# Attention: the scores of the next unit are issued ahead of a stage's product with the values

## The reference, cut to what matters

```python
# group B, 8 heads: three dilated windows (128,1), (512,4), (2048,16), each a softmax, merged
s = einsum(q, k) * SCALE;  p, lse = masked_softmax(s, mask);  o = einsum(p, v)
# group A, 8 heads in 2 groups of 4: compressed blocks, selected blocks, sliding window of 512
s = einsum(q, kc) * SCALE; p_cmp, _ = masked_softmax(s, ...);  o_cmp = einsum(p_cmp, vc)
top, idx = top_k(score from p_cmp)                             # which key blocks are looked at
s = einsum(q, ks) * SCALE; p, _ = masked_softmax(s, ms);       o_slc = einsum(p, vs)
s = einsum(q, kw) * SCALE; p, _ = masked_softmax(s, window);   o_win = einsum(p, vw)
o = g0 * o_cmp + g1 * o_slc + g2 * o_win
```

## Time and profile before

| | us |
|---|---|
| median of 3 runs | 2145.36 (2137.95 to 2154.14) |
| the profiled execution | 2156.45 |
| its span, first to last instruction | 2154.6 |
| attention: PE's first turn to its last product | 548.8 to 1160.2 |
| PE busy in the span | 1894.2 (88%) |
| DVE busy | 1111.1 (52%) |
| ACT busy | 821.7 (38%) |
| POOL busy | 272.2 (13%) |

### The profile page before, as it was taken

The page is one execution under the profiler, slowest core; times in us unless marked ns, Lnnn a source line. Parts: engine busy times, 40 slices in busy tenths (PEclk is TensorE's granted clock), DMA queues, the critical chain, the costliest instruction groups (busy, mean ns, idle before and its releaser), DMA issues. The chain is left out here.

```text
span 2154.6 us, 29729 instructions
## 1 busy us (share of the span) xinstructions
PE 1894.2 (88%) x10915; PEld 1555.6 (72%) x10915; DVE 1111.1 (52%) x2627; ACT 821.7 (38%) x1742; POOL 272.2 (13%) x342
## 2 busy tenths in 40 slices
PE   3998996457799868888884999999999999999997
PEld 3787775456688757777673778788778878878885
DVE  4776861122678757776774433443344344344344
ACT  4444431100678756665664323222123122222211
POOL 0000000101344434443431000000000000000000
PEclk9999997688899999999997999999999999999998
DMA  5322213661465523222224311220231121133102
GB/s 176 110 76 101 81 51 58 85 118 40 130 168 157 151 71 107 82 84 82 84 94 127 123 59 59 98 71 28 97 98 59 40 98 59 40 98 127 32 18 87
DMA packets 172326, 189.93 MB, mean 88 GB/s; under 512 B 55942, under 2 KB 139110, under 8 KB 171000
## 3 DMA queue, kind: packets, MB, share of 16 engines
q1 hardware_dynamic: 170114, 187.13, 29.9%
q10 hardware_dynamic: 2080, 1.05, 0.2%
HBM read 166.60 MB, written 59.81 MB: 105 GB/s over the span
## 5 line engine op out<-in xcount | busy, mean ns | idle before, releaser
L2419 DVE SCALAR_TENSOR_TENSOR m_conv<-m_ext,m_taps,m_conv 128x512 f32<-128x512 f32 x44 | 33.1, 751 | 371.7 <-ACT m_ext L2311 371.7
L1737 DVE CUSTOM_DVE_ANT_0 l_e<-l_s,k_masks 128x1024 f32<-128x1024 f32 (+3 forms) x192 | 138.4, 721 | 85.1 <-PE l_s L1382 75.3
L2161 PE MATMUL o_py<-f_h_hi,m_gu_hi 128*128 128x512 f32 x704 | 179.8, 397 | 0.0
L2161 PE MATMUL o_py<-f_h_lo,m_gu_hi 128*128 128x512 f32 x704 | 178.4, 395 | 0.0
L2161 PE MATMUL o_py<-f_h_hi,m_gu_lo 128*128 128x512 f32 x704 | 178.4, 395 | 0.0
L1679 ACT ACTIVATE l_e<-l_e,l_nmin 128x640 f32<-128x640 f32 (+11 forms) x224 | 169.9, 758 | 20.5 <-DVE l_nmin L1737 18.9
L1636 ACT ACTIVATE l_pT_hi<-l_t 128x512 fp32r<-128x512 f32 (+3 forms) x288 | 125.7, 472 | 120.7 <-PE l_t L1422 119.4
L2309 ACT ACTIVATE m_conv<-o_py,m_taps 128x512 f32<-128x512 f32 (+1 forms) x66 | 42.8, 648 | 333.2 <-PE o_py L2161 333.2
L1807 DVE TENSOR_TENSOR l_pT_lo<-l_t,l_pT_hi 128x512 fp32r<-128x512 f32 (+3 forms) x288 | 143.4, 526 | 27.1 <-ACT l_pT_hi L1636 26.6
L2161 PEld LDWEIGHTS o_py<-f_h_lo,m_gu_hi 128*128 128x128 f32 x704 | 131.9, 187 | 32.3
L2161 PEld LDWEIGHTS o_py<-f_h_hi,m_gu_lo 128*128 128x128 f32 x704 | 131.9, 187 | 32.3
(11 more groups left out here) (283 smaller groups left out, 3941.2 us busy)
## 6 DMA issues: line engine op xcount, KB each, us to landing
m_raw_gu<-in_w_gate SPq DMA_DIRECT2D x22, 512.0 KB, 5.4
m_raw_gu<-in_w_up SPq DMA_DIRECT2D x22, 512.0 KB, 7.1
m_raw_d<-in_w_down SPq DMA_DIRECT2D x11, 1024.0 KB, 5.0
p_raw<-in_w_in SPq DMA_DIRECT2D x5, 2048.0 KB, 8.0
c_rows<-in_cache_cmp SPq DMA_DIRECT2D x64, 128.0 KB
a_kd_k<-in_state_dil SPq DMA_DIRECT2D x8, 1024.0 KB, 8.3
a_kd_v<-in_state_dil SPq DMA_DIRECT2D x8, 1024.0 KB, 7.8
a_kd_k<-in_cache_slc SPq DMA_DIRECT2D x128, 64.0 KB, 1.8
```

Source lines behind the costliest of these rows:

```text
L1737: return nc.vector.tensor_tensor_reduce(out=dst, in0=src, in1=m, scale=1.0, scalar=CLAMP, op0=ALU.add, op1=ALU.min, accum_out=low)
L2161: last = nc.tensor.matmul(bank[q % 3][:, 0:w], ws[k][:, m, c, :], hs[:, c, t0:t0 + w], start=(j == 0 and c == 0), stop=(j == 2 and c == KC ...
```

## The change

TensorE's list in `attend` is written in another order. Within stage s it is now: `tr(s-3)`, the turns of s, `qk(s+1)`, `pv(s-4)`. As the stages follow each other, that is the same cycle of four parts with one exchange: the scores of unit s+1 stood behind the product with the values of unit s-4, and stand ahead of it now. `chunk_plan` follows, since "new" belongs to `qk` of unit sl. Every other engine's list is word for word the same, and no instruction is added or removed.

```diff
@@ chunk_plan
     for s in range(-1, STAGES):
-        if 0 <= s < NU and UNITS[s][0] == "sl":
-            add("new", s)
         u = s - LAG_T
...
         for e in turn[s]:
             add(*e)
+        if s + 1 < NU and UNITS[s + 1][0] == "sl":
+            add("new", s + 1)
         u = s - LAG_V
         if 0 <= u < NU and UNITS[u][0] in ("sd", "sc", "sl", "sw"):
             add("pv", u)
@@ attend, block.tensor
             for s in stages():
-                u = unit_at(s, 0)
-                if u is not None:
-                    qk(u)
                 u = unit_at(s, LAG_T)
                 if u is not None:
                     tr(u)
                 for e in turn_at[s]:
                     extra(e)
+                u = unit_at(s + 1, 0)
+                if u is not None:
+                    qk(u)
                 u = unit_at(s, LAG_V)
                 if u is not None:
                     pv(u)
```

## The result

Over 13 runs of each kernel the changed one takes 2169.67 us (2156.68 to 2181.34) and the kernel before 2157.2 us (2137.95 to 2170.73). The ratio is 1.0059, with a 95% interval of 1.0035 to 1.0083: 0.6% slower, or 12.7 us of 2157.2; the two medians lie 12.5 us apart. The 2145.36 us from which the prediction starts was the median of three runs; the wider set lies 0.55% higher, so the forecast is best read as a ratio: 2160 / 2145.4 = 1.0068 was said, 1.0059 was measured.

What follows compares the result with a forecast made beforehand. PE, the fullest engine, was taken to bound attention, so only its 85 us of waits could move. Dilated 13.5, sparse 2 and mask wait -0.5 made 15 us, taking 2145.4 to 2160 us; range 2144 to 2177.

Steps and rivals of the forecast that it cites:

- Place 1: Border between dilated passes: scores of d7 go ahead of sample sd's product, d6 starts 1.03 us later; 7 borders, 7.2 us.
- Place 2: Middle of a dilated pass: scores of d4 go ahead of d6's product and wait for DVE; 0.9 us, 8 times, 7.3 us.
- Other exchanges of a dilated pass: All remaining swaps of scores and product in a dilated pass: taken to cost or gain nothing.
- The last dilated pass swallows 1 us: Last dilated pass, which also waits for the sparse part's first keys: estimated to absorb 1 us of the loss.
- Place 3: Border between sparse passes: scores of sw and l6 go ahead of products, l7 and l6 wait; 1.8 us lost per pass.
- Places 4: Sparse passes: products that waited for their bank or turned rows get scores as cover; 1.5 us gained per pass.
- Sparse passes net 0.3 us, 2 us in all: Border loss of 1.8 us less product gains of 1.5 us per sparse pass, 7 times; bounds -12 to +14 us.
- The sum, 15 us: Whole attention: 13.5 us dilated, plus 2 sparse, less 0.5 at the first mask wait, makes 15 us slower.
- Rival 1: Scores covering the products' waits outweigh the losses, if DVE reads d5 and l7 earlier: 2140 or 2133 us; chance 0.08.
- Rival 2: Waits only change their name, each loss shortening the next wait: even, 2145 us give or take 5; chance 0.19.
- Rival 3: Lateness piles up until turns wait too, and sparse passes gain nothing: 2173 or 2181 us; chance 0.18.
- Rival 4: PE's granted clock falls after the new waits, 28 us more over 16 passes: 2188 us; chance 0.03.

Runs made afterwards that it cites:

- e5: Kernel before, with only the scores of d7 moved ahead of the product of sample sd, at the border between dilated passes: 2172.01 us in one execution.
- e6: Kernel before, with only the scores of d4 moved ahead of the product of d6, in the middle of dilated passes: 2174.28 us in one execution.
- e3: The changed kernel, but with the old order kept for the scores of d7 and d4 (dilated) and sw and l6 (sparse): 2145.21 us, ratio 0.9951 to before.
- e7: Kernel before, with only the scores of sw and l6 moved ahead of the product, at the border between sparse passes: 2163.6 us in one execution.
- e4: The changed kernel, plus DVE reading the next unit's scores ahead of its addition to `l_acc` in all stages: 2156.6 us, ratio 1.0006 to before.
- e9: The changed kernel, plus DVE reading scores ahead of its addition to `l_acc` only at the borders between passes: 2157.78 us, ratio 0.9996 to before.
- e1: Kernel before, with the scores moved ahead of the product in the dilated passes only: 2169.07 us, ratio 1.0054 to before.
- e12: Dilated passes of e3; sparse passes with scores ahead except l6, and DVE reading scores first where they are ahead: 2142.74 us, ratio 0.9933 to before.
- e11: e3, plus DVE reading the scores ahead of its addition to `l_acc` wherever they stand ahead of the product: 2150.78 us, ratio 0.9964 to before.

## Why the prediction was right

*Nothing outside attention moves; PE's waits are the stock.* Right in the main: the matmuls are the same, attention grew by 12.2 us, and the medians by 12.5. But only 8.7 us of it are in the waits of scores and products, and PE's busy time grew too, by 4.6 us.

*Place 1, 1.03 us a border.* Right in mechanism, 17% too high: e5 measures 0.88. The chain is as it was said, and the wait of 1.28 us in after was put at 1.26. The missing 0.15 us is a pause that the sum left out: the four turns of past keys (L1531) ahead of the place take 0.53 us to the next group in before (675.54 to 676.07), and 0.36 us in e5 (657.72 to 658.08), where the scores of d7 follow them in place of the sample's product. So 1.03 us of scores are 0.17 us of pause less.

*Place 2, 0.9 us a pass.* Right in mechanism, a quarter too high: e6 measures 0.7, with waits of 1.25 and 1.50 us in turns where I had 1.65. I took the end of the turn of keys from a step of 0.1 us a turn; its row says 667.26 + 0.53 = 667.79, and from there to 669.31 it is 1.52. The price at the place itself was right: counted from the start of the pass, the turn of sd (L1442), which comes next but two, starts 0.96 to 0.99 us later in e6 than in before, and 0.2 us of that is made up over the next two groups of turns (L1521, L1531). And dilated passes come in two kinds, 24.79 and 24.95 us long before, of which I had looked at one; the other pays 0.62 us.

*Other exchanges of a dilated pass, 0.* Mis-sized: e3 measures a gain of 0.37 us. One exchange gives all of it. From the turn of queries (L1515) behind the turn of d7 to the next such turn, before takes 665.47 - 661.38 = 4.09 us and e3 637.84 - 634.13 = 3.71. Between them stand the product of d2 and the scores of sd; the product waited 0.16 us for `l_acc` in before, and that wait lies under the scores now. By the runs a dilated pass costs 0.88 + 0.70 - 0.37 = 1.21 us; after shows 26.09 - 24.87 = 1.22, and I had 1.9. The whole dilated part, the mask wait included, grew by 9.9 us, where I had 13.5 - 0.5 = 13.

*The last dilated pass swallows 1 us.* Wrong in its sign. From turn of queries to turn of queries the last period grew from 27.46 to 30.85 us, 3.4 in place of some 1.2. Its one long wait for DVE, of a turn of keys (L1521) for `l_pT_lo`, grew from 1.98 to 2.94 us, and the granted clock is 0.51 from 745 to 752 us (the wait, then the window):

```profile
746.44 0.72 PE L1521 MATMUL l_t<-l_ident_r,l_k_split 128*128 128x128 f32 x4 [2.94 <-DVE l_pT_lo L1807]
```

```profile
745.00:752.00 7.00, 5.56 (x26) 5.30 (x27) 5.33 (x15) 3.65 (x8) 1.89 (x3) 0.51 0.60 178
```

In before the granted clock is 1.00 over all of 560 to 760. So some 2 us of the 9.9 come from this one pass, by the longer wait and by the clock, and none of them was in the sum.

*Place 3, 1.8 us a border.* Right in mechanism, 38% too high: e7 measures 1.3. From the taking out of sl's product to the start of l7 I had 1059.17 to 1060.71, 1.54 us; after has 1123.77 to 1125.01, 1.24 us, since DVE adds and reads with hardly a pause between. l6 waits 0.89 us where I had 1.1.

*Places 4, a gain of 1.5 us.* Mis-sized by half: e3 measures 0.7 us in an undisturbed sparse pass. The wait of l4 fell by 0.61, near the 0.7 that I gave it, and the products' waits for turned rows went from 6.8 + 6.7 = 13.5 us to 5.5, 1.0 a pass where I had 0.8. So these waits went as reckoned. An undisturbed pass of before (1057.93 to 1105.18) laid beside one of e3 (1045.19 to 1091.57) shows what took the rest back, ahead of the scores of l4; first before, then e3:

```profile
1085.47 0.50 PE L1381 MATMUL l_s<-l_kB,l_qT 128*128 128x512 f32 x1 [0.52 <-DVE l_nmin L1737]
```

```profile
1071.39 0.19 DVE L1741 COPY l_oa_s<-l_t 128x32 f32<-128x32 f32 x1 [0.44 <-PE l_t L1481]
1072.83 0.50 PE L1381 MATMUL l_s<-l_kB,l_qT 128*128 128x512 f32 x1 [0.79 <-DVE l_nmin L1744]
```

At the turn of the block choice (L1548), PE is 0.43 us ahead of before (24.74 us from the start of the pass in place of 25.17); at the scores of l4 it is 0.10 us behind (27.64 in place of 27.54). The scores of l5 now stand ahead of the small product of sample sc, DVE waits 0.44 us for that product, and only then adds and reads l5. This is place 3 over again at a fourth place, which I had counted among the harmless ones.

*Sparse passes net 0.3 us, 2 us in all.* 1.3 - 0.7 = 0.6 by the runs, 0.5 in after (47.7 - 47.2), and the part grew by 2.3 us. The net is near since both of its terms were too large by about the same: this hit was luck.

*The sum, 15 us.* 12.2 in the profile, 12.5 in the medians. With the prices of the runs it is 7 x 0.88 + 8 x 0.70 + 7 x 1.3 - 8 x 0.37 - 8 x 0.7 = 12.3. The places and the way in which each costs are as foretold; the losses of the three were put 17 to 38% too high and the gains of the sparse passes twice too high, and these errors partly cancel: the nearness of the sum is in part luck.

*The waits.* Scores were to wait some 60 us and wait 52.5; products were to wait under 15 and wait 11.1. A dilated pass was to last 26.8 and lasts 26.1, a sparse one 47.6 and lasts 47.7.

*The rivals.* Rival 1 fell as a forecast, but holds place by place: freed of the three places the same idea gains 13 us (e3). Its point of decision was that DVE reads d5 and l7 1 us earlier; e4 changes DVE's order to that end and comes out even with before. Rival 2 is out by e3 and e5 to e7, though e9 shows a border at which it is right, and the scores of l4 are another. Rival 3 asked for waiting turns; turns of `l_e` wait 9.5 us in after and 9.8 in before, so the change adds nothing there. Rival 4 was given 3% and fell in its size: the mean granted clock is 0.952 over the 13 executions of after and 0.953 over the 35 of before that went with e1 to e4. In the last dilated pass of this profile it is right. What it said of before, that the clock elsewhere is 1.00 and that the trace doesn't show it moving at short waits, is wrong (see the end). And the 12 us of the earlier trace rows lie mostly in the long wait and not behind it: from 760 to 768.5 PE is not busy at all and the clock is 0.65.

The rule of the Trainium skill ("Perfetto Trace Analysis", Matmuls) that independent groups rotate through banks is not borne out at the three places, where the next unit needs a bank of the one directly before it; the gains of 0.37 and 0.7 us a pass elsewhere agree with it. Shared banks alone don't divide the places, though: d5 needs a bank of the unit directly before it (sd) too, and its exchange is among the ones left in e3. What DVE's list has ahead of the scores decides with them.

## What to carry to other kernels

Which of two ready groups PE should issue first is decided by the list of the engine that frees their banks: follow that list to the group which it frees first, and give PE that one first. A change of issue order can cost at a few places of a loop and gain at the others: make it place by place (e3), and move the reader's order with it where a run shows that this pays (the sparse passes of e12, 45.7 us against 46.5 in e3) and not where it doesn't (the dilated ones of e11, 25.6 against 24.5). Where an edit repeats in every pass, price one pass from the timeline, then run it with one place at a time: here 1.1% (1.0059 against 0.9951) lay between the change at every place and the same change with three places left out.

## What the runs showed of the hardware that I had not expected

Some sparse passes are longer in every kernel. Two reasons show. The first is work: the periods of the passes p 10 and p 11 carry 16 transposes of keys (L1521) that the others don't have, for the second group of heads. In e7, whose clock is 1.00 in both, the period of p 10 and the one of p 12:

```profile
861.95:912.20 50.25, 43.00 (x350) 35.54 (x349) 35.85 (x114) 33.97 (x84) 21.90 (x28) 1.00 0.23 71
962.15:1010.88 48.73, 40.50 (x332) 33.73 (x331) 34.25 (x112) 30.94 (x75) 18.85 (x24) 1.00 0.29 86
```

The second reason is the clock. In the sparse part it falls in single passes of both kernels, far from any long wait. In after, the sparse pass ahead of the one shown above (47.63 us at 1.00), and two stretches in it, and the wait between them from the timeline:

```profile
1028.98:1077.38 48.40, 42.05 (x330) 34.88 (x331) 34.48 (x113) 31.17 (x76) 18.88 (x24) 0.96 0.26 83
...
1038.00:1042.00 4.00, 2.87 (x36) 2.38 (x34) 2.18 (x7) 2.43 (x6) 1.88 (x3) 1.00 0.09 27
1042.00:1046.00 4.00, 3.80 (x19) 3.10 (x20) 3.87 (x13) 3.87 (x10) 3.44 (x4) 0.57 0.48 120
```

```profile
1042.20 0.90 PE L1422 MATMUL l_t<-k_ident,l_e 128*128 128x128 f32 x3 [1.34 <-DVE l_pT_lo L1807]
```

Over 4 us the clock is 0.57, so for most of them it was granted at the lower level of 1.2 GHz. In the 4 us ahead of it PE was busy for 2.87; nearly all of the rest is the wait of 1.34 us that ends at 1042.20. The pass is 48.40 - 47.63 = 0.8 us longer. The same wait (1.31 us, at 1090.59) stands in the next pass, and there the clock doesn't fall. In before it also falls in single sparse passes, so these falls are nothing that the change brought (one of three windows of 48 us with a lower clock):

```profile
965.00:1013.00 48.00, 41.74 (x323) 35.14 (x323) 33.26 (x111) 30.34 (x74) 18.44 (x24) 0.93 0.29 87
```

What decides in which pass the clock falls was not found. So kernels were compared here by their undisturbed passes first, and by their sum second.
